# S5 part on quadrants, S5 row exchange through memory on two queues, first two chunks on unnormed operands, S5 coefficients moved

## The reference

```python
h = rmsnorm(x, norm_w)                 # x * rsqrt(mean(x^2) + eps) * norm_w
proj = h @ w_in                        # 25 chunks of 128 columns (one has only 16)
y_s5  = s5_branch(s5_u, ...)           # complex diagonal state space, 16 groups of 16 channels, 64 states
y_hg, y_gla = gated_chunk_scan(...)    # two gated linear attentions
y_ret = retention_chunk_scan(...)
x = x + concat(y_s5*silu(z0), y_hg*silu(z1), y_gla*silu(z2), y_ret*silu(z3)) @ w_out
```

## Time and profile before

| what | us |
|---|---|
| median of 3 runs | 352.05 |
| lowest and highest | 350.2 and 356.67 |
| the profiled execution, its own time | 353.67 |
| its span, first to last instruction | 351.8 |
| PE matmul busy in the span | 330.3 (94%) |
| DVE busy | 236.1 (67%) |
| ACT busy | 121.0 (34%) |
| POOL busy | 43.4 (12%) |

### The profile page before, as it was taken

How to read it: one execution, slowest core, us unless ns; L and a number is a source line. 1 busy time by engine, 2 the same in 40 slices (tenths; PEclk the granted TensorE clock), 3 DMA queues, 4 the chain that set the end, 5 groups by cost and what they waited for, 6 DMA issues and landing times.

```text
span 351.8 us, 6392 instructions
## 1 busy us (share of the span) xinstructions
PE 330.3 (94%) x2546; PEld 280.9 (80%) x2546; DVE 236.1 (67%) x501; ACT 121.0 (34%) x262; POOL 43.4 (12%) x81
## 2 busy tenths in 40 slices
PE   7899998889999999989979999999999999989991
PEld 6688876667889898869967888887888989877990
DVE  2574499986628978485749727596644897686454
ACT  4243001150691003583412620115177010566321
POOL 4018530006000000250000000000600000120000
PEclk9999999999999999899999999999999999999997
DMA  8977622232531500799915472322262242476503
GB/s 281 380 258 229 241 95 86 61 109 72 163 111 61 180 2 2 240 199 273 351 39 159 141 268 91 119 80 102 92 182 64 102 136 66 124 192 120 184 1 123
DMA packets 28013, 50.85 MB, mean 145 GB/s; under 512 B 6288, under 2 KB 6864, under 8 KB 27984
## 3 DMA queue, kind: packets, MB, share of 16 engines
q1 hardware_dynamic: 25968, 44.06, 37.9%
q0 software_dynamic: 1728, 6.29, 7.5%
q10 hardware_dynamic: 288, 0.09, 0.1%
HBM read 46.80 MB, written 3.64 MB: 143 GB/s over the span
## 4 chain that ended last, share of the span: by engine, by line
PE 75%; DVE 13%; POOL 4%; ACT 4%; issue 2%; DMA 1%; DVEq 0%; POOLq 0%; ACTq 0%
PE pr L490 41%; PE pr L764 10%; DVE att L1327 2%; PE wk L557 2%; DVE h L1059 2%; PE wk L679 2%; PE wk L504 2%; PE wk L725 2%; POOL lev L1577 2%; PE wk L602 1%; POOL lev L1579 1%; PE wk L570 1%; DMA x<-in_xt 1%; PE wk L671 1%; PE wk L617 1%
## 5 line engine op out<-in xcount | busy, mean ns | idle before, releaser
L490 PE MATMUL pr<-h,wring 128*128 128x264 f32 x768 | 178.9, 389 | 3.2 <-DVE h L1059 3.2
L490 PEld LDWEIGHTS pr<-h,wring 128*128 128x128 f32 x768 | 143.3, 190 | 30.0 <-issue 5.9
L764 PE MATMUL pr<-a_hi,w_hi 128*128 128x264 f32 x96 | 27.6, 288 | 0.0
L764 PE MATMUL pr<-a_lo,w_hi 128*128 128x264 f32 x96 | 27.2, 283 | 0.0
L764 PE MATMUL pr<-a_hi,w_lo 128*128 128x264 f32 x96 | 27.2, 283 | 0.0
L877 ACT ACTIVATE v<-pr 128x264 f32<-128x264 f32 x12 | 4.7, 388 | 48.2 <-PE pr L490 48.2
L865 ACT ACTIVATE h<-x 128x264 f32<-128x264 f32 x24 | 9.5, 420 | 32.8 <-DVE x L1480 30.7
L948 ACT ACTIVATE zs<-pr 128x264 f32<-128x264 f32 x16 | 6.0, 384 | 41.7 <-PE pr L490 41.7
L1327 DVE COPY_PREDICATED att<-masks,wk 128x512 f32<-128x512 int32 x20 | 17.6, 950 | 1.0
L764 PEld LDWEIGHTS pr<-a_lo,w_hi 128*128 128x128 f32 x96 | 18.1, 188 | 0.1
L764 PEld LDWEIGHTS pr<-a_hi,w_hi 128*128 128x128 f32 x96 | 18.1, 188 | 0.1
(11 more groups left out here) (281 smaller groups left out, 539.6 us busy)
## 6 DMA issues: line engine op xcount, KB each, us to landing
wring<-in_w_in SPq DMA_DIRECT2D x100, 256.0 KB, 3.0
wring<-in_w_out SPq DMA_DIRECT2D x20, 256.0 KB, 3.7
w_hi<-in_w_out POOLq DMA_DIRECT2D x6, 512.0 KB, 4.3
w_lo<-in_w_out POOLq DMA_DIRECT2D x6, 512.0 KB, 7.8
x<-in_xt SPq DMA_DIRECT2D x2, 528.0 KB, 4.7
out_y<-h SPq DMA_DIRECT2D x4, 264.0 KB, 2.0
s5m_t<-in_s5m SPq DMA_DIRECT2D x2, 512.0 KB, 4.4
ss<-in_hg_in SPq DMA_DIRECT2D x2, 512.0 KB, 4.0
```

Of the source, the lines that this page charges most:

```text
L490: mm = nc.tensor.matmul(ring_bank(layer, i)[:, 0:TT], wring[:, slot, n, :], act_in[:, k, :], start=(k == 0), stop=(k == KT - 1))
L764: mm = nc.tensor.matmul(ring_bank(layer, i)[:, 0:TT], w[:, j % WSLOTS, n, :], a[:, k, :], start=(k == 0 and p == 0), stop=(k == KT - 1 and ...
```

## The change

Three things that belong together, and an order of work that follows them.

1. **S5 on quadrants.** B, C and the block response are now 16 channels wide (GC = 16); every S5 product is two matmuls, one for each half of 64 partitions (rows 64g to 64g+64 in, the same rows of PSUM out). The 24 copies of `s5_relay` go; ACT takes chunks 15 and 16 out of PSUM with four copies each, by time phase (`s5_in_rows`), SP writes `u` to memory and reads it back into `ub` with 8 DMAs (`u_to_rows`). `s5_within` copies the response to `resp` and adds the skip there; SP places it into `tmat` with 8 DMAs (`block_kernel`). `s5_back` goes: the result is written to memory with 8 DMAs, four on SP's and four on ACT's queue (`y_to_rows`), and read back with one (`y_from_rows`). `yg` stays in phase order; `s5_gate` multiplies it by the gate ahead of time. `glu_gate` now comes behind chunk 24.
2. **First chunks unnormed.** `xw = x * norm_w` (in `zs`) is made before `rstd` is known; chunks 0 and 1 are products of `xw`, and DVE multiplies by `rstd` when it takes them out (`first_chunks`). `mean_square` comes in the middle of chunk 0, behind its k = 5 in layer 0 and its k = 3 in layer 1; layer 0 now sums the squares on DVE too.
3. **Coefficients later.** `s5_coefficients` and its wait for `ph_ready` stand behind the first level's scores.

```diff
@@ tiles @@
-        s5m_t = sb("s5m_t", 4, S5T, 32)
+        s5m_t = sb("s5m_t", 4, S5T, GC)
-        tmat = sb("tmat", S5T, P)
+        tmat = sb("tmat", S5T, SL * GC)
+        xw = zs
-        BANK_TURN = list(range(NCH - 1)) + [NCH, NCH + 1, NCH - 1] + list(range(NCH + 2, USES))
+        BANK_TURN = list(range(USES))
+        def y_to_rows(eng, layer, g):
+            yv = yb.rearrange("p (s k) -> p s k", s=S5T)
+            rows = y_rows[layer].rearrange("(s g c) x -> g c s x", g=2, c=GC)[g]
+            for j in range(SL):
+                at = 64 * g + GC * j
+                to, n = (SC * j + NS, SC) if j else (0, SC + NS)
+                eng.dma_start(rows[:, :, to:to + n], yv[at:at + GC, :, 0:n]).then_inc(y_out_rows, 16)
@@ SP @@
+            def u_to_rows(layer):
+                chunk_out(sp, layer, C_U1)
+                sp.dma_start(u_rows[layer].rearrange("(t p) x -> p t x", p=P), u[:, :, :]).then_inc(u_out, 16)
...
+                sp.wait_ge(u_out, 16 * (layer + 1))
+                for g in range(2):
...
+                        sp.dma_start(ub[at:at + GC, :, to], rows[:, :, src]).then_inc(u_in, 16)
+            def block_kernel(layer):
+                sp.wait_ge(resp_ready, layer + 1)
+                for g in range(2):
+                    for q in range(SL):
+                        at = 64 * g + GC * q
+                        sp.dma_start(tmat[at:at + GC, :, GC * (3 - q):], resp[64 * g:64 * g + GC, :, 0:GC * (q + 1)]).then_inc(tmat_in, 16)
+            def y_from_rows(layer):
+                sp.wait_ge(yb_ready, layer + 1)
+                y_to_rows(sp, layer, 0)
+                sp.wait_ge(y_out_rows, 16 * 8 * (layer + 1))
+                sp.dma_start(yg[:, :, :], y_rows[layer].rearrange("(t p) x -> p t x", p=P)).then_inc(yg_in, 16)
                     chunk(w_in[layer, i])
+                    if i == NCH - 3:
+                        u_to_rows(layer)
+                    if i == NCH - 1:
+                        block_kernel(layer)
-                    if i == 3 and layer + 1 < DEPTH:
+                    if i == 3:
+                        y_from_rows(layer)
+                    if i == 5 and layer + 1 < DEPTH:
                         sp.wait_ge(glu_done, layer + 1)
+                        s5_matrices(layer + 1)
@@ PE @@
+            def project_first(layer):
...
+                    scaled_by_weight(pe, layer, k)
+                    mm = nc.tensor.matmul(ring_bank(layer, C_F0)[:, 0:TT], wring[:, slot, n, :], xw[:, k, :],
+                                          start=(k == 0), stop=(k == KT - 1))
...
+                    if k == SUM_AT[layer]:
+                        mean_square(layer)
             def s5_turn(layer):
-                for r in range(4):
-                    for n in range(4):
-                        src = (bb_re, bb_im)[r // 2][:, 4 * (r % 2) + n, :, :]
-                        mm = nc.tensor.transpose(wk[:, r, P * n:P * n + P], src.rearrange("p j c -> p (j c)"), c("ident"))
+                for n, src in enumerate((bb_re, bb_im)):
+                    for s in range(S5T):
+                        for g in range(2):
+                            rows = slice(64 * g, 64 * g + 64)
+                            mm = nc.tensor.matmul(wk[rows, n, 64 * s:64 * s + 64], src[rows, s, :, :].rearrange("p j c -> p (j c)"),
+                                                  c("ident")[rows, rows], start=True, stop=True)
             def s5_inputs(layer):
-                        mm = nc.tensor.matmul(wk[:, 2 * n + s // 4, a:a + NS + SC], gtr[:, n, s, :], ub[:, s, 0:NS + SC],
-                                              start=True, stop=True)
+                        for g in range(2):
+                            rows = slice(64 * g, 64 * g + 64)
+                            mm = nc.tensor.matmul(wk[rows, 2 * n + s // 4, a:a + NS + SC], gtr[rows, n, s, :], ub[rows, s, 0:NS + SC],
+                                                  start=True, stop=True)
             def s5_outputs(layer, n):
...
+                    for k, (w, data) in enumerate(parts):
+                        for g in range(2):
+                            rows = slice(64 * g, 64 * g + 64)
+                            mm = nc.tensor.matmul(wk[rows, 4, a:a + 72], w[rows], data[rows], start=(k == 0), stop=(k == 2),
...
                 sample_outputs(layer, 1)
+                project(layer, NCH - 1)
                 glu_gate(layer)
                 ret_means(layer)
-                project(layer, NCH - 1)
@@ ACT @@
+                if n == 0:
+                    act.wait_ge(par_in, 16)
+                    for k in range(KH, KT):
+                        step(fn(xw[:, k, :], x[:, k, :], ACT.Copy, scale=par(Q_NORM + k)), xw_act)
-                evac(layer, C_F0, x3[:, 0, :])
-                evac(layer, C_LR, lr_t)
-                s5_relay(layer)
+                        act.wait_ge(yb_ready, layer + 1)
+                        y_to_rows(act, layer, 1)
-                        s5_back(layer, (2, 3))
-                        act.wait_ge(glu_done, layer + 1)
-                        step(fn(glu[:, :, :], wk[:, 0:2, 0:TT], ACT.Tanh, scale=0.5), glu_tanh)
                         negated_high(layer)
                     silu(layer, i)
...
+                act.wait_ge(glu_done, layer + 1)
+                step(fn(glu[:, :, :], wk[:, 0:2, 0:TT], ACT.Tanh, scale=0.25), glu_tanh)
@@ DVE @@
+            def first_chunks(layer):
+                for i, dst in ((C_F0, x3[:, 0, :]), (C_LR, lr_t)):
+                    dve.wait_ge(proj_done, layer * NCH + i + 1)
+                    step(tt(dst, ring_bank(layer, i)[:, 0:TT], rstd, ALU.mult), first_evac)
             dve.wait_ge(par_in, 16)
+            s5_steps()
+            for k in range(KH):
+                scale_by_weight(0, k)
+            for m in range(1, KT - 1):
+                sum_squares(0, m)
             dve.wait_ge(cst_in[0], 16)
-            s5_steps()
                 scale_x(layer, Q_NORM + layer * KT, h_ready)
+                first_chunks(layer)
...
                 level_operands(layer, 0)
-                if layer == 0:
-                    dve.wait_ge(ph_ready, 1)
-                    s5_coefficients()
...
                     level_scores(layer, n)
+                    if layer == 0 and n == 0:
+                        dve.wait_ge(ph_ready, 1)
+                        s5_coefficients()
...
-                s5_back(layer, (0, 1))
...
+                s5_gate(layer)
                 center(layer)
...
                     residual(layer, m)
+                    if layer + 1 < DEPTH and m:
+                        settle()
+                        for k in range(m if m > 1 else 0, m + 1):
+                            scale_by_weight(layer + 1, k)
```

More of the change, by code:

```diff
@@ L38 @@
 NP = NCH - NZ
+FIRST = 2
+SUM_AT = (5, 3)
 BL = 32
@@ L771, in _ @@
             for layer in range(DEPTH):
-                mean_square(layer)
                 for i in range(NCH - 1):
-                    if i == C_LR:
+                    if i == C_F0:
+                        project_first(layer)
+                    elif i == C_LR:
                         project_low_rank(layer)
@@ L938, in turned, with s5_turned @@
                         wk[:, 4, 0:n].rearrange("p (a b c) -> p a b c", a=dst.shape[1], b=dst.shape[2]), ACT.Copy), tr_evac)
-            def s5_turned(layer, rounds):
-                for r in rounds:
-                    act.wait_ge(gtr_done, layer * 4 + r + 1)
-                    step(fn(gtr[:, r // 2, 4 * (r % 2):4 * (r % 2) + 4, :].rearrange("p s m -> p (s m)"),
-                            wk[:, r, :], ACT.Copy), gtr_evac)
+            def s5_turned(layer):
+                for n in range(2):
+                    act.wait_ge(gtr_done, layer * 2 + n + 1)
+                    step(fn(gtr[:, n, :, :].rearrange("p s m -> p (s m)"), wk[:, n, :], ACT.Copy), gtr_evac)
             def silu(layer, i):
@@ L1222, in s5_within @@
                 dve.wait_ge(kt_done, layer + 1)
-                for q in range(4):
-                    for half in range(2):
-                        src = wk[32 * half:32 * half + 32, 4, :].rearrange("p (s m) -> p s m", s=4)[:, :, 0:32 * (q + 1)]
-                        step(cp(qrt(tmat, q)[:, 4 * half:4 * half + 4, 32 * (3 - q):P], src))
+                if layer == 0:
+                    dve.wait_ge(skip_in, 32)
+                for g in range(2):
+                    rows = slice(64 * g, 64 * g + GC)
+                    step(tt(skip[rows], c("ident")[rows, rows].unsqueeze(1).to_broadcast([GC, S5T, GC]),
+                            skip_w[rows, S5T * layer:S5T * layer + S5T].unsqueeze(2).to_broadcast([GC, S5T, GC]), ALU.mult))
+                    step(cp(resp[rows, :, :].rearrange("p s m -> p (s m)"), wk[rows, 4, :]))
                 settle()
-                for s in range(S5T):
-                    step(stt(out=tmat[:, s, :], in0=c("rev"), scalar=par(Q_S5D + layer * S5T + s), in1=tmat[:, s, :],
```

(6 more changed lines are left out.)

226 lines of the change are left out of this document (123 added, 103 removed).

## The result

The changed kernel took 340.63 us (median of 4 runs, 339.61 to 341.31) where the kernel before took 352.83 beside it: a ratio of 0.967, 95% interval 0.962 to 0.971. The forecast was 338, with 331 to 350 as range; the time lies in the range, between the forecast's sum (338.2) and rival (a)'s (342.4), and a little nearer to the second. The profiled execution of the changed kernel took 340.87 us (span 339.1), 12.8 less than before's 353.67, where the sum said 15.5. The ratios leave out slow executions, those over 1.5% above the fastest of their kernel: here the 356.67 of the kernel before, and further down one of e1 that took 473.31 with a granted clock of 0.65.

The account below looks back on a forecast made before the run. The prediction took PE, busy in 94% of the span, to bound the kernel. From the profiled 353.67 us its terms, -6.0 - 4.6 - 1.4 - 0.8 - 2.7 = -15.5, gave 338.2, stated as 338, range 331 to 350.

Parts of the forecast that it names:

- S5 on quadrants: S5 products in both layers: paired 64x64 passes at 32 ns each, net -2.3 us a layer, -4.6 in all.
- rival (a): Row exchanges: a hop takes 5.0 us beside the weights and `w_hi`, `y` 2.1 late in each layer; 342 us, chance 0.15.
- The levels: Layer 0 scan levels: PE waits for operands 0.4 us in all instead of 4.6, a gain of 4.2.
- The start: Start of layer 0: lower clock until some 13.5, h at 15.6, chunk 2 done at 20.3 instead of 21.9, -1.6 us.
- the change of tile shape: S5 blocks: each change costs 0.2 to 0.3 us, three or four more blocks have one, +1.0 a layer.
- Rival (b), pairs in turn: S5: quadrant pairs sharing a PSUM bank run one after the other, 61 ns a pass; 353 us, no change, chance 0.14.
- The row exchanges: DMA trips of `u`, `tmat` and `y`: 2.2 to 4 us from issue to landing, all hidden from PE.
- The tail of layer 0: From the gate's start to `w_out` tile k = 2: about 7.1 us instead of 7.8, -0.7 in each layer.
- The clock's fall at `glu_gate`: Clock drop at the gate, layer 0 alone, 1.7 us; half of it counted as gained, -0.8.
- Between the layers: From the last `w_out` product to the end of chunk 2: 9.1 us instead of 11.8, -2.7.
- Rival (c), slow hops throughout: Row exchanges: every hop takes 7.8 us, `u` 5.3 and `y` 7.7 late; 364 us, slower, chance 0.07.
- Its own signs: Signs of right: no level wait over 0.5 us, chunk 2 done by 20.3; of wrong: PE waiting ahead of `glu_gate`.

Follow-up runs that it names:

- e1: Changed kernel with the S5 coefficients and their wait for POOL's sines put back ahead of the first level: 346.53 us, ratio 0.984.
- e12: Kernel before with only the S5 coefficients moved behind the first level's scores: 354.55 us against 352.19, ratio 1.006.
- the control: The changed kernel run once more with no edit, among the follow-up runs: 340.74 us, ratio 0.969.
- e6: Changed kernel with 16 instead of 7 throwaway warm-up products ahead of chunk 0: 338.28 us, ratio 0.962.
- e10: Changed kernel with the loop over the two halves outermost in the S5 inputs, so neighbouring passes use the same quadrant: 345.21 us, ratio 0.982.
- e3: Changed kernel with all eight writes of the S5 result on SP's queue, none on ACT's: 343.36 us, ratio 0.977.
- e4: Changed kernel with ACT's third negated copy of `w_hi` put behind the logs and exponentials: 338.85 us, ratio 0.962.
- e2: Changed kernel with chunks 0 and 1 again products of the normed `h`, the mean square ahead of them: 349.88 us, ratio 0.994.
- e8: Changed kernel with four of the eight `tmat` DMAs issued by ACT instead of SP: 341.82 us, ratio 0.971.
- e9: Changed kernel with the edits of e4, e6 and e8 together: 336.34 us, ratio 0.957.

## Why the prediction was right, and where its steps failed

The profiled times, term by term of the sum (forecast, then measured): start and levels of layer 0 -6.0, -4.9; S5 in both layers -4.6, -6.9; tail and clock of layer 0 -1.5, -0.4; between the layers -2.7, -2.6; tail of layer 1 -0.7, +2.0. Together -15.5, -12.8. The first is read at PE's first turn product behind the levels (72.29 before, 67.42 now), the third what is left of the 8.7 by which tile k = 2 of `w_out` comes earlier (156.22 to 147.51) after the first and one layer's S5; the fourth is the stretch from the last `w_out` product to the end of chunk 2 (11.8 to 9.24); the last is what is left of 1.5 (127.6 to 126.1 from chunk 2 to k = 2 in layer 1) after S5.

- **The levels**: right, mechanism and size. PE waits 0.9 where 0.4 was forecast and 4.6 before. What the forecast missed is why moving the coefficients pays: e12 shows that it isn't enough with the wide `s5_c`.
- **The start**: the failed assumption is "I take the lower level until some 13.5". In the profiled execution the clock row stayed at 0.50 through all twelve passes, 5.62 us, and h came at 16.43, not 15.6: -0.8 instead of -1.6. In the control's execution h came at 15.36 and chunk 2 ended at 20.05, slightly ahead of the forecast's 15.6 and 20.3. So the assumption held in one of these two executions and failed in the other. e6, with the twelve passes at 2.91, ended chunk 2 at 19.49, 2.4 before 21.9, where the forecast's bound was 2.9; PE waited 1.0 for the sums.
- **S5 on quadrants**: "I take 32 ns a pass" was right: 31, 30, 34 and 34 ns in the four blocks. Mis-sized was the change of tile shape, +1.0: none is seen between the rows of the chain. So some -3.4 a layer (1.75 + 1.87 + 3.52 + 2 x 2.83 = 12.8 against 2.01 + 1.89 + 2.15 + 2 x 1.65 = 9.35) instead of -2.3. One slip in the price of a pass changes nothing here: 0.222 us doesn't come from the 28 passes in 6.50, which give 0.232, but from a chunk such as this one of the kernel before (chain), 3.56/16:

```profile
89.49 3.56 PE pr L490 x16
```

- **Rival (b), pairs in turn**: fell. e10 is the test: with neighbours on one quadrant the pass costs 62 ns, the forecast's 61 for two in turn, and in the change's order 34, though both halves write one PSUM bank. The rule of the Trainium skill, TensorEngine Tiling (Array Packing), Restrictions and Gotchas, that different row tiles can't access the same PSUM bank at the same time, doesn't hold for this pattern, where the two tiles write different PSUM partitions of the bank; whether it holds for the same partitions, no run here shows.
- **The row exchanges**: "I take 2.2 to 4" was right, or a little long, for `ub`, `tmat` and layer 0's `y` (1.7 to 3.2), too short for the write of `u` in layer 0 (4.8, which no PE wait followed), and too short for `yg` in layer 1: 2.65 and then 7.22. PE waited 2.5 ahead of `glu_gate`; this is rival (a)'s mechanism, in one layer of two and with 2.5 instead of 2.1. Ahead of it DVE stood 1.68 for the sample values, which waited on SP behind `tmat`: the 1 us of room that the prediction gave them was overdrawn.
- **The tail of layer 0**: the step that failed is "ACT's tanh and table load to 3.2 after the gate's start". From the gate's start to k = 2 it took 9.27 instead of 7.1, since ACT's silu of chunk 24 came at 142.11 behind copies of `w_hi`. The prediction named the DMA engines that `yg` shares with `w_hi`, but not the engine queue that waits for `w_hi`. In layer 1, where nothing of this stood in the way, the same stretch took 7.23 (299.53 to 306.76). The clock's fall at `glu_gate` didn't come in the changed kernel's profile (3.53 before, 1.94 now): 1.6 gained at the gate, where 0.8 was counted. It did come at the gate in e3 and e4 (3.49 and 3.75).
- **Between the layers**: right, 9.24 for the forecast's 9.1.
- **Rival (c), slow hops throughout**: fell; only the read back of `y` in layer 1 came near 7.8. The constant in its break-even should be 36.4 (8 x 7.8 less 26.0), not 36.6, which changes nothing.
- **Its own signs**: three that it named came out against it: a level wait over 0.5 (0.9), a wait of PE ahead of `glu_gate` (2.5), and chunk 2 done after 20.3 (21.11, but 20.05 in the control).

The total lies in the range partly by luck: two errors of size, S5 too small a gain and the tail of layer 1 a loss instead of a gain, partly cancelled. The total was 2.7 off, as much as its worst single term (2.7).

## What to carry to other kernels

Price a PE wait of several microseconds as more than its length: look in the windows for the granted clock in the few microseconds behind it, and where it fell count the work there at half speed. When a transfer or a wait is added, follow not only who needs the data but which engine's queue stands behind whatever waits for a neighbour transfer; here ACT's copies of `w_hi` held a silu that PE needed. When a small transfer shares the DMA engines with large ones, look at which is issued first. And try edits in pairs: moving the coefficients gave nothing by itself (1.002 to 1.009), and the level waits went only with both edits in.

## What the runs showed that was not expected

- Two 64x64 quadrants that write one PSUM bank run beside each other: 34 ns a pass against 62 in turn (e10).
- The clock often fell behind a wait of PE, but the wait's length doesn't decide it. It fell behind 4.7 us (e1, 0.51 over 7 us), 5.8 (e3, 0.57 over 4), 2.7 (e12, 0.57 over 4), but also behind 2.3 (e4, 0.57 over 4), and behind 1.55 between the layers in e2. It didn't fall behind 2.5 and 1.5 in the changed kernel, behind the same 1.55 in the kernel before, or in the 7 us behind the 2.9 in e10. In e12 the row was still 1.00 for 2 us after PE had resumed; in e1 it fell while PE still stood.
- Extra passes ahead of the first product kept the start fast (e6: twelve passes in 2.91, against 5.62 and 4.88 without them).
- The same 264 KB transfer took 2.8 to 4.1 us when issued ahead of `w_hi` or within 0.3 us of it, and 6.0 to 8.0 when issued 0.8 to 1.9 us behind its first piece; one of 512 KB for `w_hi` took a median of 5.8 in the changed kernel and up to 10.0 in e8. The loads of the S5 matrices (`s5m_t`), now cut out in runs of 64 bytes, took a median of 8.5 to land; PE waited for none of them. A margin under 2 us behind such a transfer can't be counted on: PE's wait for the silu was gone in e4 and back at 1.5 in e9, with the same order on ACT.
